# State-space heads: turned outputs ahead of later decays, the skip term from scaled x tiles, weight pieces split two further ahead of each group's root

## The reference

```python
xbc = jax.nn.silu(causal_dwconv(xbc, conv_w) + conv_b)
xs, bm, cm = jnp.split(xbc, (2048, 2048 + 4 * 128), axis=-1)
xh = xs.reshape(b, s, 32, 64)                       # 32 heads of 64, 4 groups
y = ssd_chunked(xh, dt, a, bm, cm)                  # two chunks of 128 tokens
y = y + d_skip[:, None] * xh                        # the skip term
yg = y.reshape(b, s, 2048) * jax.nn.silu(z)
yg = yg.reshape(b, s, 4, 512)
yg = yg * lax.rsqrt(jnp.mean(yg * yg, axis=-1, keepdims=True) + EPS)
y = (yg.reshape(b, s, 2048) * norm_g) @ w_out       # w_out: "ssm_out"
```

## Time and profile before

| | us |
|---|---|
| median of 3 runs | 1542.31 (1541.71 to 1542.85) |
| the profiled execution's own time | 1543.0 |
| its span, first to last instruction | 1541.1 |
| granted clock of PE over the span | 0.995 |

### The profile page before, as it was taken

The page is one execution under the profiler, slowest core; times in us unless marked ns, Lnnn a source line. Parts: engine busy times, 40 slices in busy tenths (PEclk is TensorE's granted clock), DMA queues, the critical chain, the costliest instruction groups (busy, mean ns, idle before and its releaser), DMA issues.

```text
span 1541.1 us, 22903 instructions
## 1 busy us (share of the span) xinstructions
PE 1512.0 (98%) x9276; PEld 1309.0 (85%) x9276; DVE 602.2 (39%) x1008; ACT 830.5 (54%) x1293; POOL 1155.7 (75%) x499
## 2 busy tenths in 40 slices
PE   9999999999999999999999999999999999999997
PEld 7888889999878898888888898888888888888886
DVE  3111016447786612331330498872113747311101
ACT  6444364375756536364554677145445376564444
POOL 8888978888758888578869796317888964388893
PEclk9999999999999999999999999999999999999999
DMA  6555555565644655255655553105555542355552
GB/s 232 192 189 192 180 191 182 178 208 185 206 151 145 198 177 196 94 203 189 191 181 192 174 193 130 50 29 192 180 187 198 194 160 77 102 178 185 191 195 79
DMA packets 71865, 259.87 MB, mean 169 GB/s; under 512 B 7984, under 2 KB 8784, under 8 KB 71504
## 3 DMA queue, kind: packets, MB, share of 16 engines
q1 hardware_dynamic: 69552, 250.97, 49.5%
q10 hardware_dynamic: 2208, 7.43, 1.3%
HBM read 257.29 MB, written 1.08 MB: 168 GB/s over the span
## 4 chain that ended last, share of the span: by engine, by line
PE 85%; DVE 8%; ACT 4%; issue 2%; POOL 1%; DMA 1%; ACTq 0%; DVEq 0%; POOLq 0%
PE bank L537 14%; PE bank L539 14%; PE bank L538 13%; PE bank L568 5%; PE bank L567 5%; PE bank L569 5%; PE bank L507 5%; PE bank L509 5%; PE bank L508 5%; PE bank L681 1%; DVE dec L2229 1%; ACT w_hi L1350 1%; DVE dec L2232 1%; PE bank L653 1%; DVE sq_mem L2057 1%
## 5 line engine op out<-in xcount | busy, mean ns | idle before, releaser
L440 POOL TENSOR_TENSOR w_lo<-raw,w_hi 128x1024 fp32r<-128x1024 f32 x468 | 1128.8, 2445 | 340.0 <-ACT w_hi L1350 339.8
L1350 ACT ACTIVATE w_hi<-raw 128x1024 fp32r<-128x1024 f32 x474 | 487.9, 1058 | 287.9 <-DMA raw<-in_w 283.7
L537 PE MATMUL bank<-w_hi,u_hi 128*128 128x512 f32 x872 | 346.5, 397 | 2.4 <-POOL w_lo L464 2.0
L539 PE MATMUL bank<-w_hi,u_lo 128*128 128x512 f32 x872 | 341.2, 391 | 0.0
L538 PE MATMUL bank<-w_lo,u_hi 128*128 128x512 f32 x872 | 340.5, 391 | 0.0
L507 PE MATMUL bank<-u_hi,w_hi 128*128 128x256 f32 x688 | 197.2, 287 | 0.0
L537 PEld LDWEIGHTS bank<-w_hi,u_hi 128*128 128x128 f32 x872 | 164.5, 189 | 36.4 <-POOL w_lo L464 2.2
L509 PE MATMUL bank<-u_hi,w_lo 128*128 128x256 f32 x688 | 194.9, 283 | 0.0
L508 PE MATMUL bank<-u_lo,w_hi 128*128 128x256 f32 x688 | 194.9, 283 | 0.0
L539 PEld LDWEIGHTS bank<-w_hi,u_lo 128*128 128x128 f32 x872 | 164.1, 188 | 35.0
L538 PEld LDWEIGHTS bank<-w_lo,u_hi 128*128 128x128 f32 x872 | 164.6, 189 | 32.6
(11 more groups left out here) (432 smaller groups left out, 2072.7 us busy)
## 6 DMA issues: line engine op xcount, KB each, us to landing
raw<-in_w SPq DMA_DIRECT2D x474, 512.0 KB, 4.5
bc<-acs_scratch ACTq DMA_DIRECT2D x8, 512.0 KB, 4.4
mem_t<-in_mem ACTq DMA_DIRECT2D x2, 1024.0 KB, 6.3
xf<-in_x SPq DMA_DIRECT2D x2, 512.0 KB, 7.0
out<-out_t SPq DMA_DIRECT2D x4, 256.0 KB, 2.7
lvl<-in_lvl ACTq DMA_DIRECT2D x1, 448.0 KB, 3.1
band<-in_band ACTq DMA_DIRECT2D x1, 256.0 KB, 6.1
tri<-in_tri SPq DMA_DIRECT2D x1, 192.0 KB, 8.4
```

What stands on the lines that cost most here:

```text
L440: nc.gpsimd.tensor_tensor(w_lo[:, q % RAW, :], raw[:, q % RAW, :], w_hi[:, q % HI, :].bitcast(F32), ALU.subtract).then_inc(split_done, 1)
L537: mm(b[:], hi[:, kt, a], w_hi[:, q % HI:q % HI + 2, c], start=kt == 0, stop=False, skip_group_check=True)
L539: m = mm(b[:], lo[:, kt, a], w_hi[:, q % HI:q % HI + 2, c], start=False, stop=kt == KT - 1, skip_group_check=True)
L1350: fn(w_hi[:, q % HI, :], raw[:, q % RAW, :], ACT.Copy).then_inc(hi_made, 1)
```

## The change

- The skip term no longer uses diagonal matrices. ACT multiplies each of the 16 x tiles (128x256) in place by its skip factors; PE transposes the scaled tiles straight into the banks of y as the first contribution (eight transposes at the head of each even step, before the wait for the decays), and the matmuls of the decays are added to them. The four matmuls at the end of every step (two passes each) are gone.
- On ACT, `y_hi` of groups 0 and 1 stands between the four small exps and the large exp of `decays(5)` and `decays(7)`; on DVE, `y_lo` of groups 0, 1 and 2 stands ahead of `decay_in` and `swish`, right behind `seg`.
- On ACT, every round casts two pieces more, up to z+2k+15. On POOL, root 0 stands after the split of piece z+15 and each later root two pieces later than before, too.

```diff
-            lows(6, P0["z"] + 14)
+            lows(6, P0["z"] + 16)
             pool.wait_ge(W["half_set"], 1)
             for g in range(4):
                 group_rstd(g)
-                lows(P0["z"] + 14 + 4 * g, P0["z"] + 18 + 4 * g)
-            lows(P0["z"] + 30, P0["wo0"] - 1)
+                lows(P0["z"] + 16 + 4 * g, P0["z"] + 20 + 4 * g)
+            lows(P0["z"] + 32, P0["wo0"] - 1)
...
+                if hg % 2 == 0:
+                    pe.wait_ge(W["skip_x"], g + 1)
+                    for c in range(2):
+                        for t in range(4):
+                            mm(quads(y_bank(g, c))[:, t, :], xbc[:, 4 * g + t, c * P:c * P + P], ident[:], is_transpose=True,
+                               start=t == 0, stop=False, skip_group_check=True)
                 pe.wait_ge(W["decay"], hg + 1)
-                pe.wait_ge(W["skip_diag"], hg + 1)
...
-                for t in range(2):
-                    for c in range(2):
-                        o = slice(256 * (hg % 2) + P * t, 256 * (hg % 2) + P * t + P)
-                        m = mm(flat(y_bank(g, c))[:, o], xbc[:, 2 * hg + t, c * P:c * P + P], diag_d[:, 2 * hg + t, :], start=False,
-                               stop=hg % 2 == 1 and t == 1, skip_group_check=True)
...
-            def decays(hg):
+            def decays(hg, between=lambda: None):
...
                     fn(d[:, hh, P:S], bc[hg % 2][:, hh, P:S], ACT.Exp, bias=cols[:, 2, 4 * hg + hh:4 * hg + hh + 1], scale=-1.0)
+                between()
                 act.wait_ge(W["seg"], hg + 1)
...
-            def skip(hg):
-
-                for t in (2 * hg, 2 * hg + 1):
-                    m = fn(diag_d[:, t, :], ident[:], ACT.Identity, scale=col("ssm_d", t))
-                m.then_inc(W["skip_diag"], 1)
+            def skip(g):
+
+                for t in range(4 * g, 4 * g + 4):
+                    m = fn(xbc[:, t, :], xbc[:, t, :], ACT.Identity, scale=col("ssm_d", t))
+                m.then_inc(W["skip_x"], 1)
...
-                    decays(k + 3)
+                    decays(k + 3, (lambda: y_hi(k // 2 - 1)) if k in (2, 4) else lambda: None)
                 after(q0 + 2 * k + 7)
                 if k in (2, 4):
                     evict("z", k // 2 + 1, z)
                 if k == 6:
                     evict("gate_b", 0, sgb)
-                if k % 2 == 0 and k >= 2:
-                    y_hi(k // 2 - 1)
+                if k == 6:
+                    y_hi(2)
+                after(q0 + 2 * k + 9)
...
                 if k % 2 and k < 7:
                     y_norm(k // 2)
+                if k in (2, 4, 6):
+                    y_lo(k // 2 - 1)
                 if k + 3 < NHG:
                     decay_in(k + 3)
                 if k in (2, 4):
                     swish(k // 2 + 1)
                     dve.wait_ge(row_free, G0["z"] + k + 4)
-                if k % 2 == 0 and k >= 2:
-                    y_lo(k // 2 - 1)
```

More of the change, by code:

```diff
@@ L222, in build @@
         dec = [place("dec", [P, 4, 384], F32, kb_) for kb_ in (HB + 38, WB + 56, WB + 62)]
-        diag_d = place("diag_d", [P, 16, P], F32, WB + 16)
         mm_hi = place("mm_hi", [P, KT, S], F32R, WB + 24)
@@ L306, in build @@
                   "still_set", "first_low", "ffn_act", "ffn_t", "ffn_hi", "ffn_lo", "short_act", "short_cv", "conv_tap", "conv_first", "conv_act", "short_hi",
-                  "short_lo", "row_step", "scratch", "bc_landed0", "bc_landed1", "seg", "seg_exp", "decay", "skip_diag", "y_mm", "y_gated",
+                  "short_lo", "row_step", "scratch", "bc_landed0", "bc_landed1", "seg", "seg_exp", "decay", "skip_x", "y_mm", "y_gated",
                   "g_sq", "g_ms", "g_rs", "z_tanh", "seg_raw", "half_set", "g_n", "y_t", "y_hi", "y_lo", "mg_part", "merged", "mg_t", "m_hi", "m_lo", "at_score",
@@ L856, in y_heads @@
                     b0, b1, d = flat(y_bank(g, 0)), flat(y_bank(g, 1)), dec[hg % 3]
-                    first = hg % 2 == 0 and hh == 0
+                    last = hg % 2 == 1 and hh == 3
                     for p0 in (0, 64):
                         a = slice(p0, p0 + 64)
-                        mm(b0[a, o], d[:, hh, p0:p0 + 64], x_dt[:, g, 0, o], start=first, stop=False, skip_group_check=True)
+                        mm(b0[a, o], d[:, hh, p0:p0 + 64], x_dt[:, g, 0, o], start=False, stop=last, skip_group_check=True)
                     for p0 in (0, 64):
                         a = slice(p0, p0 + 64)
-                        mm(b1[a, o], d[:, hh, P + p0:P + p0 + 64], x_dt[:, g, 0, o], start=first, stop=False, skip_group_check=True)
+                        mm(b1[a, o], d[:, hh, P + p0:P + p0 + 64], x_dt[:, g, 0, o], start=False, stop=False, skip_group_check=True)
                     for p0 in (0, 64):
                         a = slice(p0, p0 + 64)
-                        mm(b1[a, o], d[:, hh, S + p0:S + p0 + 64], x_dt[:, g, 1, o], start=False, stop=False, skip_group_check=True)
-                for t in range(2):
-                    for c in range(2):
-                        o = slice(256 * (hg % 2) + P * t, 256 * (hg % 2) + P * t + P)
-                        m = mm(flat(y_bank(g, c))[:, o], xbc[:, 2 * hg + t, c * P:c * P + P], diag_d[:, 2 * hg + t, :], start=False,
-                               stop=hg % 2 == 1 and t == 1, skip_group_check=True)
+                        m = mm(b1[a, o], d[:, hh, S + p0:S + p0 + 64], x_dt[:, g, 1, o], start=False, stop=last, skip_group_check=True)
                 m.then_inc(W["y_mm"], 1)
@@ L1640, in _ @@
             decays(1)
-            for hg in range(4):
-                skip(hg)
+            for g in range(2):
+                skip(g)
             after(q0 + 5)
             decays(2)
-            for hg in range(4, NHG):
-                skip(hg)
+            for g in range(2, 4):
+                skip(g)
             after(q0 + 7)
```

## The result

The changed kernel took 1546.12 us (median of 10 runs, 1544.77 to 1549.04), the kernel before 1542.55 beside it. The ratio is 1.0024 with a 95% interval of 1.0016 to 1.0032: slower by 2.5 to 4.9 us. The forecast was 1547.0. The profiled execution's span went from 1541.1 to 1544.7.

A forecast was written before the change was run, and what follows sets the result against it. PE, busy 1512.0 of 1541.1 us, was taken as the bound: only its work or stalls count. +4.2 at the last turn plus 0.5 for the clock, +4.7 on 1542.3, gave 1547.0 us; 8-in-10 range 1535.5 to 1550.5.

The forecast's parts named there:

- The sum: At PE's exit from the last turn: 497.3 against 493.1 in the kernel before, +4.2 us.
- The walk: Round-by-round forecast of ACT, DVE, POOL and PE times through the stage, ending with PE's exit from `y_turn(3)` at 497.3.
- The order's gain: With `y_lo` right behind `seg`, step 4 starts at 450.9 against 452.75; 1.9 us ahead up to step 6.
- The skip term: In odd steps PE loses 7.4 us of L870 work, transposes add 3.9: 3.5 us less; saving-nothing rival 0.03.
- The loss at groups 2 and 3: Late roots and norm halves waiting on splits turn 1.9 us ahead at step 6 into +4.2 at the last turn.
- the stalls: PE's waits before turn 0, steps 4 and 6, turns 2 and 3: 0.6 + 2.0 + 3.0 + 4.1 + 2.7 = 12.4 us.
- The check by PE alone: Stage stalls of 12.4 us against 5.3 before, minus 3.5 of PE work: +3.6 us, agreeing with +4.2 within edges.
- The clock: Each new stall of 2 us or more may bring 1.7 us of slow clock; 0.5 taken, ends 0 and 3.4.
- 0 beyond the last turn: In `ssm_out` behind the last turn the order is as before, so no further gain or loss: 0.
- The start of DVE's rounds: All of DVE's rounds start 0.8 us later, delayed by ACT's longer second scalings of the x tiles.

The follow-up runs named there:

- e4: The kernel before with only the new order of the turned outputs (`decays`, `y_hi`, `y_lo`): 1540.98 us, ratio 0.9988.
- e3: The kernel before with only the new skip term by scaled and transposed x tiles: 1543.28 us, ratio 1.0001.
- e5: The changed kernel with POOL's roots where they were before, ACT's early casts kept: 1545.77 us, ratio 1.0016.
- e1: The changed kernel without the pieces ahead (no extra casts on ACT, POOL's roots as before): 1540.88 us, ratio 0.9985.
- e2: The kernel before with only the pieces ahead (extra casts on ACT, roots two pieces later on POOL): 1552.28 us, ratio 1.0054.
- e8: The changed kernel with POOL's roots as before and the norm read from PSUM, early casts kept: 1537.06 us, ratio 0.9964.

## Why the prediction was right

**The sum held at its own place.** The walk put PE's exit from the last turn at 497.3; it left at 496.81, where the next matmul starts. Its stations, forecast against measured: end of `seg(4)` 439.5 and 438.96; norm 0 440.3 and 439.82; step 4 450.9 and 450.64; norm 1 458.6 and 459.29; step 6 470.4 and 470.11; halves of norm 2 done 480.6 and 483.2, the transposes behind them at 480.06 and 482.54; norm 3 491.6 and 491.26. Against the kernel before, the exit was forecast 4.2 us later and came 3.7 later (493.08 there).

**The order's gain** was put at 1.9 us by step 6 and came out at 2.2 (470.11 against 472.33); e4 shows that it is a gain of its own.

**The skip term**: the row of eight took 1.03 to 1.09 (1.21 at step 6, at the slow clock), and the page counts 9244 matmuls, 32 fewer than before, as 64 passes went and 32 came. But 3.5 us of work were not worth 3.5 us of time; e3 shows them fully turned into waits.

**The loss at groups 2 and 3** came where the walk had it, each half of the norm after one split. e5 shows that the root's place is only part of the cause, which the text had not separated: it took each late norm from a root queued behind two splits and did not ask what the casts do if the root comes early. Had only the queue been undone, the time would have been the same. For the whole change the forecast stands, since both causes were in it.

**Sized wrong: the stalls.** The check by PE alone summed 12.4 us; measured were 3.9 + 5.4 = 9.3. The walk had 0.6 us before turn 0 where none was, 3.0 before step 6 where 1.96 were, and 4.1 before turn 2 where 2.0 were: PE came later to the last two than assumed, by the 0.85 before turn 1, put at none, and by the slow clock behind step 6. Of the 2 us for each half at turns 2 and 3 only the second halves show 1.83, the first 0.17 and 0.76. Since DVE set the pace, the exits did not move. But that the check came out at +3.6, near the walk, was luck. With the measured waits and the one slow stretch it gives 9.3 + 1.7 - 5.3 - 3.5 = +2.2, while from the scores to the matmul behind the last turn the stage took 99.05 us for 95.46, 3.6 longer. The missing 1.4 us are in no wait of the profile; where they lie was not followed.

**The clock.** The text gave 0.5 us to a slow clock behind the last turn. There was one slow stretch in the stage, behind the wait before step 6, and it cost nothing, because PE would have waited for the norm anyway. It lies here, in the changed kernel (columns as in the earlier trace rows):

```profile
470.90:474.30 3.40, 3.40 (x52) 3.00 (x51) 3.30 (x5) 1.61 (x4) 3.23 (x2) 0.51 0.51 206
```

**Given back later.** At the next marks of `ssm_out` the changed kernel stands 4.2 us behind (516.44 against 512.24, where PE sums the memory's squares) and 3.6 behind at the turn of the merged branches. In the kernel before PE waited 1.12 us there, in the changed one 0.39, as these two starts show (before, then after):

```profile
534.40 1.09 PE L922 MATMUL bank<-ident,y_a 128*128 128x128 f32 x8 [1.12 <-DVE y_a L2317]
```
```profile
537.97 1.09 PE L921 MATMUL bank<-ident,y_a 128*128 128x128 f32 x8 [0.39 <-DVE y_a L2318]
```

The prediction had 0 beyond the last turn. Measured, 0.5 us more were lost up to 516.44 and 0.6 given back behind it, so the spans differ by 3.6 where the forecast had 4.7: the exit of the last turn came 0.5 earlier than forecast, and the 0.5 for a slow clock behind it did not come. The medians are 3.6 apart, too.

**The start of DVE's rounds** was put 0.8 us later for the longer scalings on ACT; it was 0.27 (the gate at 432.76 against 432.48), of which 0.14 was there at the scores. The scalings were as long as foreseen (3.31 us for 2.45). But the later casts moved POOL's splits too, and L2233 of `seg(2)` began 0.12 us ahead of one (413.87, the split 413.99), took 0.69 us instead of 2.77, and let ACT begin its second scalings 0.6 earlier (417.39 against 417.99). That was luck:

```profile
413.87 0.69 DVE L2233 TENSOR_SCALAR dec<-dec 128x1024 f32<-128x1024 f32 x1
```

## What to carry to other kernels

Before moving DMA-fed preparation on GpSimd ahead, list which VectorE operations on SBUF data will then run beside it: here each waited for the whole split in progress, so a chain of short ones was stretched most (0.88 to 5.15 us). Put work ahead only where the other engine has nothing of that kind to do, or let the short operations read PSUM (1.41 us beside the same splits). And where a stage is paced by a chain over three engines, as here, work taken off a TensorE that shows 98% busy can be worth nothing until that chain is shorter (e3).

## What the runs showed of the hardware that was not expected

The same stall does not always bring the slow clock. In the changed kernel PE stood still for 1.96 us before step 4 and again for 1.96 before step 6; behind the first the granted clock stayed at 1.00 (the row here), behind the second it read 0.51 (above).

```profile
450.60:454.00 3.40, 3.36 (x59) 3.01 (x60) 3.37 (x4) 2.39 (x4) 1.88 (x1) 1.00 0.91 298
```

In e5 two waits of 1.83 us were each followed by the lower clock, while the two of 1.83 in the changed kernel were not. In e1 a wait of 1.84 was:

```profile
445.60:448.80 3.20, 3.20 (x9) 2.44 (x8) 2.95 (x6) 2.74 (x5) 1.30 (x1) 0.50 0.38 152
```

At the program's beginning, where this change does nothing, the traces of e1 and of e4 differ in the same way behind waits of 2.02 and 2.01 us, at 18.9 to 20.3 and 18.0 to 22.5 us:

```profile
18.90:20.30 1.40, 1.40 (x4) 1.11 (x5) 0.00 (x0) 1.31 (x2) 1.40 (x2) 0.50 0.94 375
```
```profile
18.00:22.50 4.50, 3.46 (x15) 2.85 (x16) 0.31 (x1) 4.17 (x6) 4.50 (x4) 1.00 0.56 219
```

e4 has no slow stretch there and e1 has one, and PE's first matmul of the scores, still ahead of the change, starts at 396.14 in e4 and at 397.45 in e1. So it is in all twelve traces: the six with a slow stretch at the beginning (before, after, e1, e2, e3, e8) have this matmul at 397.45 to 398.00, the six without at 396.06 to 396.32. So two traces of kernels that do the same up to there can differ by 1.3 us and more, and medians of several runs decide, or lengths inside one trace. What decides between the two is not shown by these runs.
